# Moving one tile's residual matmuls from before the mixture of experts into its first expert

## What is computed

```
h = h + hybrid_mixer(rmsnorm(h, g_mix_norm[l]), ...)
h = h + memory_cross_attention(rmsnorm(h, g_xattn_norm[l]), ...)
h = h + moe_ffn(rmsnorm(h, g_moe_norm[l]), w_router[l], b_router[l], w_gate_up[l], ...)
return rmsnorm(h, g_final)

logits = (xt @ w_router + b_router)          # moe_ffn: per token
top_v, top_e = lax.top_k(logits, TOP_K);  gate = softmax(top_v)
gu = xb @ w_gate_up[e] + b_gate_up[e]        # per expert e, for its tokens
out = ((clip(u) + 1) * (g * sigmoid(1.702 * g))) @ w_down[e] + b_down[e]
y[token] += out * gate
```

## Time and profile before

| | us |
|---|---|
| median of 3 runs | 1217.55 |
| lowest and highest of them | 1215.74, 1218.3 |
| profiled execution, its own time | 1218.37 |
| its span from the first instruction to the last | 1216.6 |
| TensorE busy | 1127.3 (93% of the span) |
| VectorE busy | 307.7 (25%) |
| ScalarE busy | 224.2 (18%) |
| moved by DMA | 445.49 MB, mean 366 GB/s |

### The profile page before, as it was taken

How to read it: one execution, slowest core, us unless ns; L and a number is a source line. 1 busy time by engine, 2 the same in 40 slices (tenths; PEclk the granted TensorE clock), 3 DMA queues, 4 the chain that set the end, 5 groups by cost and what they waited for, 6 DMA issues and landing times.

```text
span 1216.6 us, 12721 instructions
## 1 busy us (share of the span) xinstructions
PE 1127.3 (93%) x5426; PEld 493.6 (41%) x5427; DVE 307.7 (25%) x700; ACT 224.2 (18%) x451; POOL 36.2 (3%) x34
## 2 busy tenths in 40 slices
PE   6998889999999999999999999899999989999896
PEld 5886665555333333333333333333333333333332
DVE  4778562214112211111221111111111111111111
ACT  5674462242001000000110000000000000000001
POOL 0000050040000000000000000000000000000000
PEclk9999999999999999999999999999999999999998
DMA  8823433388999999999999999999999999999994
GB/s 351 300 90 149 129 139 138 108 346 311 428 429 428 426 429 428 427 427 430 426 427 429 428 427 427 428 427 428 427 429 426 428 428 427 428 428 428 427 426 185
DMA packets 44153, 445.49 MB, mean 366 GB/s; under 512 B 6048, under 2 KB 10240, under 8 KB 19424
## 3 DMA queue, kind: packets, MB, share of 16 engines
q1 hardware_dynamic: 41952, 444.37, 87.7%
q10 hardware_dynamic: 2144, 0.30, 0.2%
HBM read 443.60 MB, written 1.05 MB: 365 GB/s over the span
## 4 chain that ended last, share of the span: by engine, by line
PE 59%; DMA 32%; DVE 5%; ACT 3%; issue 1%; SPq 0%; DVEq 0%; ACTq 0%
DMA R<-in_w_gate_up 21%; PE ps L1891 19%; PE ps L1900 13%; DMA XMT<-in_w_gate_up 7%; PE ps L1756 5%; PE ps L1408 4%; PE ps L1920 3%; DMA XM<-in_w_gate_up 3%; PE ps L1867 3%; PE ps L1428 2%; PE ps L1430 2%; PE ps L1429 2%; PE ps L1662 1%; PE ps L1882 1%; ACT A L859 1%
## 5 line engine op out<-in xcount | busy, mean ns | idle before, releaser
L1891 PE MATMUL ps<-R,convT 128*64 128x512 f32 x1232 | 274.7, 594 | 25.8 <-DMA R<-in_w_gate_up 25.8
L1335 DVE TENSOR_SCALAR A<-ps 128x512 f32<-128x512 f32 x32 | 22.1, 691 | 695.0 <-PE ps L1891 695.0
L1891 PEld LDWEIGHTS ps<-R,convT 128*64 128x64 f32 x1232 | 85.3, 137 | 202.9 <-issue 149.3
L1900 PE MATMUL ps<-R,A 128*64 128x512 f32 x608 | 134.8, 592 | 0.0
L854 ACT ACTIVATE A<-A 128x512 f32<-128x512 f32 x32 | 20.2, 630 | 508.1 <-DVE A L1335 508.1
L1900 PEld LDWEIGHTS ps<-R,A 128*64 128x64 f32 x608 | 42.8, 137 | 78.2 <-issue 76.7
L1920 PE MATMUL ps<-A,convT 64*128 64x512 f32 x256 | 63.6, 615 | 1.4 <-ACT A L861 1.4
L861 ACT COPY A<-ps 128x512 f32<-128x512 f32 x32 | 18.7, 585 | 237.8 <-PE ps L1900 237.8
L1867 PE MATMUL ps<-H,convT 128*64 128x512 f32 x256 | 60.4, 592 | 0.3 <-DVE convT L1290 0.3
L1891 PE MATMUL ps<-XMT,convT 128*64 128x512 f32 x208 | 47.0, 593 | 3.7 <-DMA XMT<-in_w_gate_up 3.7
L1891 PE MATMUL ps<-QK,convT 128*64 128x512 f32 x208 | 47.0, 594 | 2.5 <-DMA QK<-in_w_gate_up 2.4
(11 more groups left out here) (301 smaller groups left out, 1206.2 us busy)
## 6 DMA issues: line engine op xcount, KB each, us to landing
R<-in_w_gate_up SPq DMA_DIRECT2D x77, 2048.0 KB, 40.8
R<-in_w_down SPq DMA_DIRECT2D x38, 2048.0 KB, 43.3
QK<-in_w_gate_up SPq DMA_DIRECT2D x13, 2048.0 KB, 40.8
A<-in_w_gate_up SPq DMA_DIRECT2D x13, 2048.0 KB, 40.8
XMT<-in_w_gate_up SPq DMA_DIRECT2D x13, 2048.0 KB, 42.2
XM<-in_w_gate_up SPq DMA_DIRECT2D x12, 2048.0 KB, 42.3
XM<-in_w_down SPq DMA_DIRECT2D x7, 2048.0 KB, 44.7
QK<-in_w_down SPq DMA_DIRECT2D x7, 2048.0 KB, 43.2
```

The lines of the kernel that those rows point to most:

```text
L1891: last = mm(bank(b)[s * SLOTS:(s + 1) * SLOTS, :], xg[:, 4 * (j % 2) + 2 * c + j // 2, :], w[:, c * 2 * FF + at + s * BANK:c * 2 * FF + at ...
L1900: last = mm(bank(O_BANK)[s * SLOTS:(s + 1) * SLOTS, :], hTm[:, c, i * SLOTS:(i + 1) * SLOTS], w[:, c * D + s * BANK:c * D + (s + 1) * BANK ...
```

## The change

`y_start(0)` is taken out from behind `router(1)` and put in front of `y_start(1)` in the first expert. Both tiles' output banks are then started there, one behind the other. Nothing is added or left out.

```diff
                 eight_transposes("h2T", 1, H[:, 1, :])
                 keep_warm(4)
                 router(1)
-                y_start(0)
 
                 pe.wait_ge(dve_g, 1)
                 pe.wait_ge(pool_moe, 8)
@@
                         gather(selx).then_inc(m_gath, 1)
                     if k == 0:
+                        y_start(0)
                         y_start(1)
                         pe.wait_ge(dve_flg, 1)
```

## The result

The changed kernel takes 1222.15 us (median of 6 runs, 1219.84 to 1222.97), the kernel before 1217.32 us (median of 6, 1215.42 to 1218.3). The ratio is 1.0038, 95% interval 1.0028 to 1.0047: slower by 4.8 us, outside the range given and on the side that had 13% of the chance. The profiled execution took 1222.03 us with a span of 1220.3 us, 3.7 us longer than the span of before.

The account below looks back on a forecast made before the run. The stream of fills was taken to set the end from 300 us on. Saving 0 in the router stage, adding 0.4 us to the stream, tail unchanged, gave 1217.9 us on the median of 1217.55 us; range 1215.7 to 1220.6 us.

Parts of the forecast that it names:

- The removal saves nothing: Router stage: taking out y_start(0) saves 0, since the third count still waits for VectorE until 289.43 us.
- 1.8 us lies nearer to 1.44 than to 3.01, so I expect the full clock: Router stage: TensorE's new idle time of some 1.8 us was expected to leave its clock at full.
- the sign of being wrong that the prediction set itself: Router stage: a granted clock below 1.00 anywhere between 287 and 300 us would show the prediction wrong.
- The rival: Router stage: TensorE's clock falls in the gap; one fall costs up to 1.7 us; chance 0.11 up to 2 us, 0.07 more.
- I take 0.4: First expert: fill 14, issued 1.72 us later, lands 0.4 us later and delays the stream of fills by that.
- the whole addition reaches the stream: First expert: fill 14 takes 9.0 us again, the stream shifts by 1.72 us, 1219.3 us; chance 0.12.
- Fill 15 and its successors add nothing: First expert onward: later fills are issued while another is under way, so they add no delay.
- A delay of TensorE alone is repaid: Early experts: a delay of TensorE alone is repaid at 658 us, where it waits less for a fill.

Follow-up runs that it names:

- e2: Kernel before with y_start(0) taken out of the router stage and put behind the first expert's last down fill: 1220.30 us against 1217.47 us.
- e6: Changed kernel with ten matmuls nobody reads in TensorE's idle time in the last expert: 1219.40 us (kernel before: 1217.82 us).
- e9: Kernel before with y_start(0) replacing the six warm-up matmuls behind the counts, its place behind the router left empty: 1220.16 us against 1217.61 us.
- e1: Kernel before with one more y_start(0) in the first expert, the router stage's kept: 1218.42 us against 1217.47 us.
- e3: Changed kernel with keep_warm(6) where y_start(0) stood in the router stage: 1219.32 us (kernel before: 1217.47 us).
- e4: Kernel before with keep_warm(6) in place of y_start(0), which moves behind the first expert's last down fill: 1218.34 us against 1217.47 us.
- e10: Changed kernel with keep_warm(3) behind router(1), leaving a gap of 1.01 us: 1219.56 us (kernel before: 1217.61 us).
- e7: Kernel before with two more y_start(0) in the first expert, the router stage's kept: 1221.06 us against 1217.82 us.
- e8: Kernel before with y_start(1) also moved from the first expert to the router stage, and ten matmuls in the last expert: 1215.51 us against 1217.82 us.

## Why the prediction was wrong

**The removal saves nothing: right.** The third count starts 0.03 us from its old time, behind VectorE.

**"1.8 us lies nearer to 1.44 than to 3.01, so I expect the full clock": wrong, and this is the step that failed first.** The gap came out at 1.68 us, 0.24 us longer than one that the trace of before has at full clock, and the clock fell in each of the four profiles that have it (changed, e2, e6, e9); it fell in none of the eight with matmuls in its place. So the sign of being wrong that the prediction set itself, a clock below 1.00 between 287 and 300 us, came true. Comparing lengths of single gaps was the wrong measure, and the trace of before could have said so. It holds a gap of 2.36 us, in a part that all kernels share, behind which the clock stayed at 1.00. In e1 the same gap in front of the same matmuls was followed by a fall, as in eight more of the twelve profiles (line, then the stretch from 98 to 102 us; before, then e1):

```profile
97.86 0.50 PE L1428 MATMUL ps<-XMT_p 128*128 128x512 f32 x1 [2.36 <-DVE R_p L917]
98.00:102.00 4.00, 3.77 (x34) 2.43 (x38) 4.00 (x9) 1.27 (x2) 0.00 (x0) 1.00 0.00 0
97.32 0.50 PE L1428 MATMUL ps<-XMT_p 128*128 128x512 f32 x1 [2.36 <-DVE R_p L917]
98.00:102.00 4.00, 4.00 (x21) 2.05 (x23) 3.97 (x10) 1.27 (x2) 0.00 (x0) 0.57 0.00 0
```

The length of a gap doesn't decide, then, and neither do the instructions around it alone: one kernel's clock falls at a place in one execution and may not in the next. What sets the router stage's gap apart isn't shown. The gap of 1.44 us lay among dense matmuls of 256 and 128 columns; this one has on both sides matmuls of 32 columns, and TensorE's rows hold only 1.03 us of busy time in the 2.50 us up to 290.5 us. That this is what counts is argued from these rows, and that the clock of e9 fell half a microsecond after TensorE went idle, before the gap was over, speaks for it; what is shown is that 1.6 us of useless matmuls in the gap undo the effect (e3, e4). The Trainium skill, page "TensorE: Matmul & The Clock Gate", Part 1, has activity releasing the throttled clock, and the experiments agree. The rival had the mechanism, the place and 1.7 us as the price of one fall; it was given a chance of 0.18 where four profiles of four had the fall. Its price is 1.28 us in two profiles (changed, e2) and 2.7 us in two others (e6, e9), by how long the clock stays low.

**"I take 0.4" for the stream of fills: the step was right, its size wrong.** It measured 1.5 us (1.36 to 1.70 us in the changed kernel, e1, e3, e6 and e10). I compared a fill's landing with that of a lone fill, 7.7 us, and took the difference to the landing before. Fill 14 did land 7.9 us after its issue in the changed kernel, near the floor assumed, yet the stream was 1.5 us late by the wait near 682 us. In e1, with the same late issue, it took 9.0 us, as before, and the stream's loss was the same. In the changed kernel fill 14 landed 0.6 us later behind fill 10's issue than before, and fill 19 landed 1.6 us later (54.5 us instead of 52.9 us): when one fill lands doesn't tell when the engines are free for the next. For this kernel the experiments say: the slack at fill 14 was about 0.2 us (0 to 0.4 us by the five kernels), and beyond it a late issue is lost in full (e7). The rival "the whole addition reaches the stream", 1219.3 us, was nearer than the forecast. Its argument, that fills 13 and 14 landed 5.6 us apart because the queue was thin, falls with e8: with fill 14 issued 0.85 us earlier the time doesn't change. "Fill 15 and its successors add nothing" holds in the changed kernel as far as the rows tell; but 1.7 us of work put in front of fill 16's release (e2, e4) cost 0.4 to 0.5 us, so there too the slack is small.

**A delay of TensorE alone is repaid: right** (e4 waits first at 682 us instead of 658 us; the last waits follow the stream).

**The sum.** In the profiled execution 1.28 + 1.46 us, with 0.04 us ahead of the router stage and 0.06 us of drift of the stream, move the last wait by 2.84 us; the end adds 0.86 us. With the longer fall of e6 in place of the shorter one, the first two terms are 2.7 + 1.5 = 4.2 us. The median's 4.8 us lies above that. The two halves of the change tried alone moved the medians by 0.95 us (e1) and 2.8 us (e2), e1 and e9 together by 3.5 us. The intervals of these ratios are 1 to 1.5 us to either side, so the sum agrees within them. But 0.6 to 1.3 us of the 4.8 us, by which of these sums one takes, isn't traced to a row. The lower mean clocks of the changed kernel's runs make more time at the low clock likely, where it lies isn't shown, and how often each length of the low clock occurs stays open.

## What to carry to other kernels

Work that looks free because its engine waits anyway may be what holds TensorE's clock up. Before moving it out of a thin stage of small matmuls, put warm-up matmuls in its place, and look for idle gaps elsewhere (filling the one in the last expert was worth 2 us). One profile at full clock doesn't show that a gap is safe: look at several executions. When a stream of transfers sets the end, find the one release that it waits for closest: there the slack is the distance from the issue to the moment when the engines run out of data, not to a landing, and everything added ahead of that release beyond the slack costs its full length.

## What the runs showed of the hardware that was not expected

Two kernels that are alike up to the last expert (the changed one and e6) had the low clock for some 3 us in one execution (291 to 294 us) and about twice as long in the other (from before 289 to 295 us), so what one gap costs varies by a factor of two, 1.3 to 2.7 us. And a gap of 2.34 to 2.37 us early in the kernel, between the same instructions in all twelve, was followed by the low clock in nine profiles and by the full clock in three (before, changed, e10). A stream of transfers that ran dry took microseconds to come back to its 427 GB/s: in e7 it moved 229 and 115 GB/s in the two microseconds behind the standstill.
